# Query sums of the decode samples in a retention layer: four matmuls in four column groups, and one turn per head

## The reference, cut to what matters

```python
def step(s, inp):
    qc, kc, vc = inp
    a = jnp.einsum('bnhk,bmhk->bhnm', qc, kc) * decay
    o = (jnp.einsum('bhnm,bmhv->bnhv', a, vc)
         + jnp.einsum('bnhk,bhkv->bnhv', qc, s) * xi[None, :, :, None])
    s = g_c[None, :, None, None] * s + jnp.einsum('bmhk,bmhv->bhkv', kc * zeta[None, :, :, None], vc)
    return s, o
...
mu = jnp.mean(o, axis=-1, keepdims=True)
var = jnp.mean(jnp.square(o - mu), axis=-1, keepdims=True)
o = (o - mu) * lax.rsqrt(var + GN_EPS)
o = o.reshape(B, L, hv) * jax.nn.silu(g.astype(jnp.float32))
```

## Time and profile before

| | |
|---|---|
| time, median of 3 runs | 1894.39 us (1893.44 to 1895.09) |
| profiled execution, its own time | 1892.95 us |
| its span, first to last instruction | 1891.2 us |
| TensorE busy | 1805.9 us, 95% of the span |
| VectorE busy | 1041.9 us, 55% |
| ScalarE busy | 911.6 us, 48% |
| GpSimd busy | 774.0 us, 41% |
| mean granted TensorE clock | 0.982 |

### The profile page before, as it was taken

How to read it: one execution, slowest core, us unless ns; L and a number is a source line. 1 busy time by engine, 2 the same in 40 slices (tenths; PEclk the granted TensorE clock), 3 DMA queues, 4 the chain that set the end, 5 groups by cost and what they waited for, 6 DMA issues and landing times.

```text
span 1891.2 us, 32237 instructions
## 1 busy us (share of the span) xinstructions
PE 1805.9 (95%) x13996; PEld 1731.5 (92%) x13996; DVE 1041.9 (55%) x1124; ACT 911.6 (48%) x1064; POOL 774.0 (41%) x225
## 2 busy tenths in 40 slices
PE   8999989999979999899999978999999999999997
PEld 7999989999969999888989868999999998999997
DVE  4454555675386753545555555676244545467743
ACT  4555555444454444444444445443455565544443
POOL 4554535555314444322122101455364454444441
PEclk9999989999989999999999989999999999899999
DMA  8767854555424556745545522455668667545552
GB/s 271 248 221 267 282 197 145 180 177 175 148 90 158 179 184 197 224 158 165 164 140 164 156 78 90 156 178 164 212 205 288 222 231 271 180 134 179 180 182 85
DMA packets 306035, 346.31 MB, mean 183 GB/s; under 512 B 7847, under 2 KB 269479, under 8 KB 305887
## 3 DMA queue, kind: packets, MB, share of 16 engines
q1 hardware_dynamic: 257968, 260.36, 43.4%
q10 hardware_dynamic: 47927, 83.90, 12.7%
HBM read 299.66 MB, written 44.82 MB: 182 GB/s over the span
## 4 chain that ended last, share of the span: by engine, by line
PE 82%; DVE 9%; ACT 4%; issue 3%; DMA 1%; ACTq 1%; PEldq 0%; DVEq 0%
PE acc L1491 21%; PE acc L1492 20%; PE acc L1498 20%; PE mix L1631 2%; PE mix L1889 2%; PE mix L1553 1%; PE acc L1519 1%; ACT w_hi L433 1%; PE acc L1520 1%; DVE w_lo L925 1%; PE acc L1525 1%; PE mix L1643 1%; PE mix L1862 1%; PE mix L1720 1%; DMA st<-in_state_ret_dram 1%
## 5 line engine op out<-in xcount | busy, mean ns | idle before, releaser
L1398 POOL TENSOR_TENSOR w_lo<-raw,w_hi 128x2048 fp32r<-128x2048 f32 (+2 forms) x162 | 690.2, 4265 | 688.9 <-ACT w_hi L433 688.9
L1491 PE MATMUL acc<-g_hi,w_hi 128*128 128x264 f32 x2544 | 639.8, 289 | 8.6 <-DVE gate L1182 2.9
L1492 PE MATMUL acc<-g_lo,w_hi 128*128 128x264 f32 x2544 | 628.9, 284 | 0.0
L433 ACT ACTIVATE w_hi<-raw 128x2048 fp32r<-128x2048 f32 (+3 forms) x260 | 455.8, 1755 | 162.3 <-PE acc L1498 79.2
L925 DVE TENSOR_TENSOR w_lo<-raw,w_hi 128x2048 fp32r<-128x2048 f32 (+2 forms) x98 | 381.0, 3888 | 266.7 <-ACT w_hi L433 266.7
L1491 PEld LDWEIGHTS acc<-g_hi,w_hi 128*128 128x128 f32 x2544 | 479.4, 188 | 18.5 <-issue 13.7
L1492 PEld LDWEIGHTS acc<-g_lo,w_hi 128*128 128x128 f32 x2544 | 482.0, 189 | 1.3
L1498 PE MATMUL acc<-g_hi,w_lo 128*128 128x264 f32 x2544 | 343.7, 285 | 0.6 <-POOL w_lo L1398 0.6
L1498 PEld LDWEIGHTS acc<-g_hi,w_lo 128*128 128x128 f32 x2544 | 325.9, 188 | 3.6 <-issue 1.3
L1431 POOL TENSOR_TENSOR h_lo<-hid,h_hi 128x528 fp32r<-128x528 f32 x44 | 59.2, 1345 | 332.7 <-ACT h_hi L707 332.7
L704 ACT ACTIVATE silu_gate<-gate 128x528 f32<-128x528 f32 x44 | 28.4, 646 | 283.6 <-DVE gate L1182 283.6
(11 more groups left out here) (241 smaller groups left out, 2400.1 us busy)
## 6 DMA issues: line engine op xcount, KB each, us to landing
raw<-in_w_ffn_in_dram SPq DMA_DIRECT2D x88, 1024.0 KB, 5.3
raw<-in_w_in_ret_dram SPq DMA_DIRECT2D x48, 1024.0 KB, 6.9
raw<-in_w_in_attn_dram SPq DMA_DIRECT2D x36, 1024.0 KB, 5.7
st<-in_state_ret_dram ACTq DMA_DIRECT2D x64, 512.0 KB, 6.7
out_dram<-st ACTq DMA_DIRECT2D x64, 512.0 KB, 6.1
raw<-in_w_ffn_out_dram SPq DMA_DIRECT2D x32, 768.0 KB, 4.3
raw<-in_w_ffn_out_dram SPq DMA_DIRECT2D x32, 640.0 KB, 4.6
raw<-in_w_out_ret_dram SPq DMA_DIRECT2D x16, 1024.0 KB, 6.7
```

Of the source, the lines that this page charges most:

```text
L433: A(w_hi[:, u % SPL, 0:size[u]], raw[:, u % RAW, 0:size[u]], ACT.Copy).then_inc(hi_split, 1)
L1398: TT(w_lo[:, u % SPL, 0:size[u]], raw[:, u % RAW, 0:size[u]], w_hi[:, u % SPL, 0:size[u]].bitcast(F32), ALU.subtract).then_inc(lo_by_pool, 1)
L1491: MM(out, wh, x_hi[:, ks[k], :], start=first and k == 0, stop=False)
L1492: MM(out, wh, x_lo[:, ks[k], :], start=False, stop=False)
```

## The change

The stationary operand of the query sums becomes an 8-column window of a new 15-column table `one_of`, which is zero but for a column of ones in its middle: for sample b the window has its ones in column b. The moving operand is a 128-column block of `tq`. Four such matmuls go to four column groups of 32 (their `tile_position`), and write 8 rows each at partitions 0, 32, 64 and 96, adding over the 8 samples of a head. The 8 x 512 outputs of a head so lie as rows, and are brought into the transposed layout once per head: ScalarE copies 128 x 128 from PSUM to `o_rows` (`sample_rows`), TensorE turns it (`turn_samples`), and ScalarE copies 8 of each 32 columns to `oT` (`sample_out`). At s = 4, `turn_samples` stands behind the second part of `proj`, `gn_mean` behind the whole unit, and ScalarE does `hi(ub + 6)` before `sample_rows`. After the last head the three steps move likewise.

```diff
-    base = np.zeros((P, 2 * P + 2), np.float32)
+    base = np.zeros((P, 2 * P + 17), np.float32)
...
+    base[:, 2 * P + 9] = 1.0
...
+        one_of = tbase[:, 2 * P + 2:2 * P + 17]
...
+            o_rows = sb("o_rows", [P, P], F32, s)
...
+                def sample_rows(gh):
+                    act.wait_ge(qs_done, 8 * (gh + 1))
+                    A(o_rows[:], mix[:, 0, 0:P], ACT.Copy, scale=1.0 / 16).then_inc(o_rows_ready, 1)
+
                 def sample_out(gh, par):
-                    act.wait_ge(qs_done, 8 * (gh + 1))
-                    A(oT[:, par, :, SEQ:T], mix[:, 0, 0:32].rearrange("p (v b) -> p v b", v=4), ACT.Copy,
-                      scale=1.0 / 16).then_inc(os_ready, 1)
+                    act.wait_ge(os_turned, gh + 1)
+                    A(oT[:, par, :, SEQ:T], mix[:, 0, P:2 * P].rearrange("p (v r) -> p v r", v=4)[:, :, 0:DECB],
+                      ACT.Copy).then_inc(os_ready, 1)
...
+                    hi(ub + 6)
                     if h:
+                        sample_rows(gh - 1)
                         sample_out(gh - 1, 1 - par)
-                    hi(ub + 6)
...
+                sample_rows(gh)
                 ro_split(3)
                 sample_out(gh, 1)
...
                     for vt in range(4):
-                        ins = MM(mix[:, 0, vt * 8 + b:vt * 8 + b + 1], tq[:, vt * P:(vt + 1) * P], ones[:, 0:1],
-                                 start=True, stop=True)
+                        ins = MM(mix[32 * vt:32 * vt + DECB, 0, 0:P], one_of[:, 7 - b:15 - b], tq[:, vt * P:(vt + 1) * P],
+                                 start=(b == 0), stop=(b == 7), tile_position=(0, 32 * vt))
                     ins.then_inc(qs_done, 1)
+
+                def turn_samples(gh):
+                    pe.wait_ge(o_rows_ready, gh + 1)
+                    TR(mix[:, 0, P:2 * P], o_rows[:], ident).then_inc(os_turned, 1)
...
                         elif h and s == 4:
-                            samples = (lambda: query(8 * h - 1), None, lambda: gn_mean(h - 1))
+                            samples = (lambda: query(8 * h - 1), lambda: turn_samples(gh - 1))
...
                             if h:
+                                gn_mean(h - 1)
                                 pe.wait_ge(st_updated, 32 * r + 8 * h)
...
                 proj(uo + 3, po + 1, ro_hi, ro_lo, pieces[0], first=False, last=False, done=False,
-                     between=(lambda: gn_mean(3, True), None, lambda: gn_variance(3, True)))
+                     between=(lambda: turn_samples(RH * r + 3), lambda: gn_mean(3, True)))
+                gn_variance(3, True)
```

More of the change, by code:

```diff
@@ L224, in trunk @@
         prev_hi, prev_lo = g_hi_all[:, :, T:T + DECB], g_lo_all[:, :, T:T + DECB]
-        tbase = sb("tbase", [P, 2 * P + 2])
+        tbase = sb("tbase", [P, 2 * P + 17])
         gains = sb("gains", [P, KD, 18])
@@ L340, in trunk @@
         st_stored = [sem(f"st_stored{i}") for i in range(ST)]
-        st_scaled, sel_ready, vb_done, st_updated, t_first_ready, t_ready, qs_done, os_ready = (
-            sem("st_scaled"), sem("sel_ready"), sem("vb_done"), sem("st_updated"), sem("t_first_ready"),
-            sem("t_ready"), sem("qs_done"), sem("os_ready"))
+        st_scaled, sel_ready, vb_done, st_updated, t_first_ready, t_ready, qs_done, o_rows_ready, os_turned, \
+            os_ready = (sem("st_scaled"), sem("sel_ready"), sem("vb_done"), sem("st_updated"), sem("t_first_ready"),
+                        sem("t_ready"), sem("qs_done"), sem("o_rows_ready"), sem("os_turned"), sem("os_ready"))
         a_done, at_ready, tk_done, kz_ready = sem("a_done"), sem("at_ready"), sem("tk_done"), sem("kz_ready")
```

## The result

The changed kernel takes 1927.58 us (median of 4 runs, 1926.48 to 1928.74), the kernel before beside it on the same chip 1893.91 us (1893.23 to 1895.09). The ratio is 1.0177, 95% interval 1.016 to 1.0195: 33.7 us slower. The forecast was 1896 with a range up to 1902.5, so it missed, and by more than its slow rival allowed.

A forecast was written before the change was run, and what follows sets the result against it. TensorE's list was taken as the bound (82% of the chain), with states, loads and ScalarE close beside it in heads 2 and 3. Terms: 3.5 + 0.6 - 2.6 = 1.5 us slower, 1896 us forecast, range 1886 to 1902.5.

The forecast's parts named there:

- slow rival: TensorE's granted clock falls to 0.50 behind waits at the turn: 4.8 to 8.1 us slower, up to 1902.5; chance 0.18.
- gn_mean behind the unit* costs nothing: Unit s = 4: moving gn_mean behind the low part is the same TensorE work before the turns of v, no cost.
- some 0.7 us early for `gn_variance`: gn_center, gn_square and gate activations come some 1.7 us later, covered by TensorE work, still 0.7 us ahead of need.
- The query's price: Each query sum on TensorE falls from 0.81 to 0.42 us, 0.4 us saved per query.
- Four groups side by side: Query matmuls in column groups overlap; if they didn't, a query costs 0.81 or more: 3.1 us slower, 1897.5.
- Heads 2 and 3 rigid: Queries 6 and 7 can come only 0.2 us earlier; what the first six save becomes waiting.
- Head 1: TensorE is the later engine there; low part starts 0.5 to 3.3 us earlier, taken as 1.3, twice: 2.6 gained.
- The turn: Before the low part, TensorE waits for ScalarE's copy behind hi(ub + 6): 3.5 us lost over four heads.
- TensorE starts the low part 2.9 us after `kz` started: Heads 1 to 3: from ScalarE's kz through rounding, copy, hand-over and turn to the low part, 2.9 us.
- The clock: Rival: turn waits of 1 us or more bring clock 0.50 in two to four heads, 4.8 to 8.1 slower; chance 0.18.
- After the last head: Copy, turn and hand-overs added before the resumption, less a shorter last query: 0.3 us later, twice, 0.6 lost.

## Why the prediction was wrong, step by step

**The step that failed** is "*gn_mean behind the unit* costs nothing", with its `gn_center` "some 0.7 us early for `gn_variance`". It priced TensorE's own work and how late `gn_center` comes, and took `gn_first` at its old 0.7 us. It took 4.3, so TensorE waited 2.84 to 2.86 us in each of six heads, lost 3.2 to 4.1 from the low part to the turns of v, and in four of them also the clock. The new place of `gn_mean` by itself shows no cost (1892.26 against 1890.43 with it back in the middle); what was put at nothing is the wait for its input. I had read what stands behind `hi(ub + 6)` on ScalarE, but not whom that rounding releases: GpSimd, which went from 1.78 us behind the start of `gn_first` to 0.81 ahead of it. The Trainium skill (SBUF — State Buffer, section "SBUF: two separate sides") states that a VectorE instruction with both inputs in SBUF and a GpSimd one that reads SBUF exclude each other through a port that they share, and that the later one is blocked for the whole of the other. The trace agrees: the addition ended 0.57, 0.56 and (128 x 16) 0.03 us after GpSimd whether it began 0.81, 0.10 or 0.72 us behind it. No run here gave `gn_first` an input in PSUM.

The trace of the kernel before showed this already, and I had overlooked it. Its line of `q_xi`, a VectorE multiplication of 128 x 256 with both inputs in SBUF, and one of the eight beside GpSimd:

```profile
L1101 DVE TENSOR_TENSOR q_xi<-rq,tret x8: 413/1743/4726, 38.0 to 1567.2; 128x256 f32<-128x256 f32 x8
...
145.05 4.60 POOL L1398 TENSOR_TENSOR w_lo<-raw,w_hi 128x2048 fp32r<-128x2048 f32 x1 [4.43 <-ACT w_hi L433]
...
148.19 1.74 DVE L1101 TENSOR_TENSOR q_xi<-rq,tret 128x256 f32<-128x256 f32 x1
```

One of the eight meets no GpSimd instruction and takes 0.41 us. The other seven start 0.15 to 4.13 us behind one, take 0.75 to 4.73 and end 0.28 to 0.29 us after it, whatever their start. It isn't for two inputs alone: the copy of 128 x 16 from SBUF to SBUF that makes `k_s` (L1096) takes 0.17 us in four heads and 1.13 to 1.15 in the four in which it starts beside GpSimd. One shape with durations this far apart in one line is the sign to look for.

**The query's price** was right within 0.1 us: 0.42 forecast, 0.34 from its start to the `spread` behind it, where it was 0.81, so the old form was the dearer one. Four groups side by side, as forecast; the wide form at 0.96 confirms it.

**Heads 2 and 3 rigid**: right. From the first to the last query of a head it was 26.9 us in each of these four heads before, and 27.4, 26.2, 26.9 and 27.6 after, though each query is 0.47 cheaper. In head 2 of the changed kernel `tq` of sample 6 ends at 158.03 + 0.75 = 158.78, and query 6 starts at 158.84; query 7 has waited 0.28 us for its own. Three quarters of the query removed gave some 5 us in all. The small stores show why.

**Head 1**: forecast 1.3 us earlier at the low part. Query 0 to query 7 took 99.80 - 73.32 = 26.48 before and 96.78 - 72.69 = 24.09 after; query 0 to the low part 29.31 and 28.23, 1.1 less. In layer 3 it was 29.31 and 28.78, 0.5 less. So 1.6 us in all instead of 2.6, the mechanism as forecast.

**The turn**: the step "TensorE starts the low part 2.9 us after `kz` started" measured 100.92 - 98.15 and 166.33 - 163.56, 2.77 both, and the same in the other four heads. What was off is where `kz` stands: in head 2 it came 1.9 us behind query 7 (163.56 against 161.67) instead of 0.6, as the scaling of a state ahead of it waited 1.76 us for a load. In the six heads it came 1.2 to 1.9 us behind query 7, before 0.6 ahead to 1.2 behind, and the low part came 4.0 to 4.7 behind query 7 instead of 2.83, together 8.6 us more. So this term was mis-sized too. It was 3.5 us for four heads; the two runs that differ in ScalarE's order and not in the collision are 11 us apart, though GpSimd's own wait is in that number too.

**The clock**: the rival had it fall behind the turn. In the changed kernel TensorE's longest wait there was 2.04 us, and the half-clock stretches begin only 5 to 6 us after the turn (100.83 and 106.9, 166.25 and 171.7), at the longer wait for `gn_first`, which the rival didn't know of. The rival's mechanism exists all the same: in the run in which GpSimd waits, one of six turns (layer 3's head 2) came after a wait of 2.06 us, and the low part behind it ran mostly at 0.50 (0.57 in the mean of 1525.0 to 1528.3) and took 3.45 us instead of 2.18.

**After the last head**: 0.3 us forecast. The rows of the changed kernel for the last query and the resumption:

```profile
285.07 0.41 PE L1640 MATMUL mix<-tq,tbase 128*8 128x128 f32 x8 [0.81 <-DVE tq L1057]
...
293.80 0.59 PE L1500 MATMUL acc<-ro_hi,w_hi 128*128 128x264 f32 x1 [1.53 <-DVE ro_lo L1155]
```

From the last query to the resumption it was 278.92 - 271.57 = 7.35 us before and 293.80 - 285.07 = 8.73 after, 1.4 later. The held late addition explains 0.6 of it: it took 1.66 us, but 1.06 before, as it met GpSimd there too. In layer 3 it took 0.27 us (0.64 before), and the distance was 9.07 us against 9.23, no later. So the term was 1.2 us in all instead of 0.6; the other 0.8 us of layer 0 wasn't taken apart.

Added up: 26 us of collision with what it does to the clock, 11 of ScalarE's order, less 3 of cheaper queries. The collision was in no term of the sum, and the turn's term was too small; together they are the miss. What stays open is how the 11 divide between the turn's wait, the clock behind it and GpSimd's.

## What to carry to other kernels

When an instruction is moved, follow what it releases on the other engines as well as what stands behind it, and look which of them will then run side by side. A VectorE addition or multiplication with two SBUF inputs that starts during a long GpSimd subtraction cost up to the whole of it here, so let the short one go first; operations with an input in PSUM were not held, but moving one there wasn't tried. Before the move, look in the old profile for one line and shape whose longest duration is several times its shortest. Where two engines' chains have nearly the same length, an edit to one is worth a few us; test by shortening the other.

## What the runs showed that I had not expected

- VectorE's 128 x 528 float32 addition took 0.71 us alone and 4.3 to 5.0 beside a 4.5 us GpSimd subtraction; a 128 x 16 one 0.18 alone and 1.66 beside one of 2.35. `update`, with one input in PSUM, took 0.74 us with and without GpSimd beside it.
- The kernel before had seven such collisions of `q_xi` and two of the late addition, of up to 4.3 us each.
- TensorE's granted clock fell to 0.50 within or just behind four of six equal waits of 2.84 to 2.86 us, and not behind the other two; the stretches lasted 3.3 to 6.7 us. It also fell behind one wait of 2.06 us in the run in which GpSimd waits.
- Cutting the stores of the states to a quarter changed the kernel before by nothing that can be measured, and the one with the new queries by 10.7 us (12 by their ratios to the kernel before).
